# A two-layer hybrid decoder trunk on one core: four reorderings at the joints between stages

## The chip, the core and the metric

The kernel runs on one core of a Trainium2 chip. A core has five engines with their own instruction streams: TensorE (PE in the profile; its weight loads are listed as PEld), VectorE (DVE), ScalarE (ACT), GpSimd (POOL) and SyncE (SP, which here only issues DMAs). They are coupled by semaphores alone. The metric is the device time of one execution in microseconds (us); lower is better.

## The reference

One sequence of 256 tokens with 1024 channels passes through two layers. Each layer is a token mixer and then a channel mixer:

```
h = rms_norm(x) * (1 + scale) + shift
z = h @ w_in                      # conv, stick-breaking q k v, gated linear q k v g, gates
y = g_a * conv(z) @ w_conv_out + g_b * stick(z) @ w_sb_out + g_c * (gla(z) * silu(gg)) @ w_gla_out
x = x + gate * rms_norm(y @ w_o)
x = x + gate * rms_norm(ffn(h2))  # layer 0: dense SwiGLU; layer 1: top-2 of 8 SwiGLU experts
```

The three branches a, b and c are the convolution, the stick-breaking attention and the gated linear attention (GLA). Each is projected to 1024 channels, multiplied by its sigmoid gate, and the three are added ("merged").

## The kernel before

**Products.** Every weight arrives in fp32 as a "unit" of 128 x 2048 values (1 MB), in the order of one list (`plan`, lines 79 to 110), through six raw buffers. ScalarE rounds a unit into a high part (`write_hi`, line 593), VectorE subtracts to get the low part (`write_lo`, line 1002), and TensorE multiplies high weights with high and low activations and low weights with high activations: 48 matmuls of 256 columns, about 5.5 us a unit. A unit's low part is needed only after its first 32 matmuls in most helpers (`low_last`); `project_merged`, which computes the first unit of `w_o`, needs it at once (`begin`). The rounded parts have few slots, so `write_hi` of a unit waits until TensorE is done with an earlier unit.

**Order of a mixer.** Units of one layer's mixer have places i: 0 to 29 are the input projection, 30 to 35 the branch projections ("out", two halves a branch), 36 to 39 `w_o`. Every engine walks the places in its own stream. At place i ScalarE and VectorE first prepare the weights of unit i + 1, and then run a `hook(layer, i)`, where the rest of the mixer's work is placed by hand. At place i VectorE also merges the out unit i - 1 (`merge`, line 1240; `MERGES`): two products of a PSUM bank with the gates (line 1253), and for branch c two further additions into the sum (line 1257). At places 35 and 36 the merge stands ahead of the weights. GpSimd adds the products of branch a to those of branch b, in four pieces q = 0 to 3 (line 568), each as soon as its products are read; the additions of branch c wait for that piece. Pieces 0 and 1 belong to the first halves of the branches, 2 and 3 to the second. ScalarE then rounds merged pieces (line 663), VectorE computes their low parts (line 1304), and TensorE's unit 36 takes them piece by piece (line 1652). Branch c's low and high parts (`split` after the product of line 1299) must be there before TensorE's first unit of branch c; that is the semaphore `c_split`.

**GLA.** At place 21 VectorE cumulates the decays, ScalarE then computes three exponentials (lines 762 to 764), and `gla_decay` (lines 1211 to 1214) multiplies with them; TensorE turns the result at place 23 (line 1852). Between them stand the convolution's taps: at each place up to 26 VectorE adds up to six of them (line 1177). At place 25 VectorE chains the states and TensorE computes GLA's output from them (line 1878).

**Dense layer.** Units are numbered from 0: gate 0, up 0, gate 1, up 1, down 0, ... Units 0 to 2 begin before the norm's scale is known, so VectorE scales units 0 and 1 later (`scale_unit`, line 1134). There are three PSUM banks for such units, so unit 3 needs the bank that `scale_unit` of unit 0 reads.

**Experts.** Eight expert steps of 42 units each. At a step's end TensorE turns the last activations (line 2062), ScalarE rounds them (line 952), VectorE computes their low part (line 1473), and TensorE runs the last two `down` units (line 2050), 24 matmuls of 512 columns. After the eighth step the results are scattered to tokens, normed and stored.

Of the kernel before, what the change touches and what calls it, by code (L numbers as in the profile page):

```python
# [30 lines left out]
P = 128  # L31
# [23 lines left out]
FT = D_FFE // 512  # L55
EU = 6 * FT
# [25 lines left out]
def plan():  # L82
# [4 lines left out]
    for layer in range(DEPTH):  # L87
        later = [("ada", 0, 1, k) for k in range(KC)] + [("ada", 0, 2, k) for k in range(4)]
        for u in range(FIRST if layer == 0 else 0, Z_UNITS + G_UNITS):
            units.append(("z", layer, u, 0))  # L90
            if layer == 0 and u in ADA_AFTER:
                units.append(later.pop(0))
        for b, h in ((1, 0), (1, 1), (0, 0), (0, 1), (2, 0), (2, 1)):
            units.append(("out", layer, b, h))
            if layer == 0 and (b, h) == (1, 0):
                units.append(later.pop(0))
# [109 lines left out]
def program(nc, x_t, vecs, c_row, glr_w, a2, router, stream, experts, out_t):  # L206
    with ExitStack() as ctx:
# [371 lines left out]
        def _(act):  # L579
# [155 lines left out]
            def hook(layer, i):  # L735
# [64 lines left out]
                if i == 31:  # L800
                    for j in range(3):
                        wait_read(act, ("z", layer, Z_UNITS + G_UNITS - 1 - j, 0))
                if i in (31, 32, 34):
                    b = {31: 1, 32: 0, 34: 2}[i]
                    g = gates[:, 8 * b:8 * b + 8, :]
                    act.activation(g, g, ACT.Sigmoid).then_inc(gates_ready, 1)
# [183 lines left out]
        def _(dve):  # L990
# [268 lines left out]
            def hook(layer, i):  # L1259
# [13 lines left out]
                if i == 25:  # L1273
                    gla_states(layer)
                if (4 if layer else FIRST + 1) <= i < 26:
                    taps(layer, i)
# [3 lines left out]
                if i == 21:  # L1280
                    gla_cum(layer)
                if i == 22:
                    gla_decay(layer)
                if i == 27:
# [7 lines left out]
                if i == 30:  # L1292
# [3 lines left out]
                    split(br_hi[0], br_lo[0], conv_tmp, a_split, layer + 1)  # L1296
                if i == 32:
                    dve.wait_ge(gg_silu, layer + 1)
# [41 lines left out]
            for layer in range(DEPTH):  # L1340
# [20 lines left out]
                if layer == 0:  # L1361
                    for i, u in enumerate(FFN_UNITS):
                        if i == 1:
                            finish_mixer_out(0)
                            finish_ffn_in(0)
                            split_shift(layer, SH_F)
                        take(u)
                        if i == 1:
# [3 lines left out]
                        if i == 3:  # L1372
                            scale_unit(FFN_UNITS[0], silu_g[0])
                            scale_unit(FFN_UNITS[1], prod[0])
# [194 lines left out]
        def _(pe):  # L1569
# [469 lines left out]
            def down(step, k, odd, half, t, first=False, last=False, rounds=0):  # L2039
# [17 lines left out]
                mm.then_inc(consumed, 1)  # L2057

            def turn(step, odd, t):
                pe.wait_ge(act_done, step * FT + t + 1)  # L2060
# [37 lines left out]
            def expert_step(step, expert, first=False, again=False, ahead=True):  # L2098
# [18 lines left out]
                if ahead:  # L2117
                    gather(step + 1, 0)
                    gather(step + 1, 1)
                pe.wait_ge(ae_split, step * FT + FT)  # L2120
                for half in range(2):
                    down(step, EU - 2 + half, 0, half, FT - 1, last=True)

# [120 lines left out]
```

## Time and profile before

| | us |
|---|---|
| three executions | 1782.36, 1782.52, 1784.28 |
| their median | 1782.52 |
| the profiled execution, its own time | 1784.1 |
| its span from the first to the last instruction | 1782.4 |
| PE busy | 1757.6 (99%) |
| DVE busy | 1522.5 (85%) |
| ACT busy | 1136.3 (64%) |
| POOL busy | 185.8 (10%) |

The profiled execution's own time is 1.7 us more than its span. Durations below come from it. A row of a timeline gives the start and the length, then engine, line, operation and tiles, how many instructions it merges, and in brackets how long the engine sat idle before it and what released it. Starts of consecutive operations of one engine are closer than their lengths, because the end of one overlaps the start of the next.

### The profile page before, as it was taken

What the parts mean: (1) busy time and instruction counts of PE and PEld (TensorE: products, weight loads), DVE (VectorE), ACT (ScalarE), POOL (GpSimd) and SP (SyncE); (2) the same over time, 40 slices, a digit from 0 to 9 for tenths busy, and PEclk for the clock granted to TensorE, in tenths of its full rate; (3) what the DMA queues carried; (4) which work ended last, traced back from release to release, by engine and by line L of the source; (5) the groups of instructions that cost most, each with busy time, mean ns of one, the idle gap of its engine ahead of it and who ended that gap; (6) DMA issues with size and microseconds to landing.
All of it is one profiled execution on the core that took longest, in us unless ns stands there. A gap on an engine that the chain in (4) does not pass through costs nothing.

```text
span 1782.4 us, 28675 instructions
## 1 busy us (share of the span) xinstructions
PE 1757.6 (99%) x10853; PEld 1557.2 (87%) x10854; DVE 1522.5 (85%) x1444; ACT 1136.3 (64%) x968; POOL 185.8 (10%) x158
## 2 busy tenths in 40 slices
PE   9999999999999999999999999999999999999997
PEld 7999999999999999968888888888888888888885
DVE  7899888999777784769898898898888988988986
ACT  5556476333464556567777777777777776777774
POOL 0395010000029400100000000000000000000000
PEclk9999999999999999999999999999999999999999
DMA  9854655999734343539989989899899899898992
GB/s 386 316 186 160 225 179 217 356 380 375 301 142 166 136 149 142 194 137 361 374 341 372 367 336 382 337 363 371 331 372 376 324 377 369 332 378 341 360 372 96
DMA packets 72820, 524.91 MB, mean 295 GB/s; under 512 B 8145, under 2 KB 8273, under 8 KB 9122
## 3 DMA queue, kind: packets, MB, share of 16 engines
q1 hardware_dynamic: 72578, 523.51, 76.8%
q8 instruction: 61, 1.00, 0.2%
q0 software_dynamic: 160, 0.23, 0.0%
q14 instruction: 21, 0.17, 0.0%
HBM read 522.65 MB, written 1.05 MB: 294 GB/s over the span
## 4 chain that ended last, share of the span: by engine, by line
PE 90%; DVE 5%; ACT 2%; issue 1%; DMA 1%; SPq 0%; DVEq 0%; ACTq 0%
PE bank L2033 34%; PE bank L1635 19%; PE bank L2050 17%; PE bank L1760 3%; PE bank L1717 3%; PE bank L1732 3%; PE bank L2072 2%; PE bank L2062 1%; PE bank L1582 1%; PE bank L1693 1%; DVE w_lo L1002 1%; DVE arena L1177 1%; DVE arena L1253 1%; ACT w_hi L593 1%; DMA raw<-in_stream 1%
## 5 line engine op out<-in xcount | busy, mean ns | idle before, releaser
L1315 DVE TENSOR_TENSOR w_lo<-raw,w_hi 128x2048 fp32r<-128x2048 f32 x224 | 509.8, 2291 | 80.2 <-ACT w_hi L842 79.6
L842 ACT ACTIVATE w_hi<-raw 128x2048 fp32r<-128x2048 f32 x224 | 429.4, 1917 | 99.6 <-PE bank L2050 70.5
L2033 PE MATMUL bank<-acts 128*128 128x512 f32 x1248 | 304.3, 393 | 0.0
L2033 PE MATMUL bank<-w_hi,acts 128*128 128x512 f32 x960 | 297.4, 391 | 0.0
L1315 DVE TENSOR_TENSOR acts<-raw,acts 128x2048 fp32r<-128x2048 f32 x112 | 256.2, 2288 | 21.1 <-ACT acts L842 20.5
L2033 PEld LDWEIGHTS bank<-acts 128*128 128x128 f32 x1248 | 231.3, 188 | 46.7 <-DVE acts L1315 0.4
L842 ACT ACTIVATE acts<-raw 128x2048 fp32r<-128x2048 f32 x112 | 215.0, 1920 | 72.3 <-PE bank L2033 69.9
L2050 PE MATMUL bank<-w_hi,acts 128*128 128x512 f32 x832 | 256.6, 390 | 0.0
L1002 DVE TENSOR_TENSOR w_lo<-raw,w_hi 128x2048 fp32r<-128x2048 f32 x82 | 190.9, 2328 | 41.1 <-ACT w_hi L593 40.8
L593 ACT ACTIVATE w_hi<-raw 128x2048 fp32r<-128x2048 f32 x82 | 156.6, 1912 | 95.1 <-PE bank L1635 66.8
L2033 PEld LDWEIGHTS bank<-w_hi,acts 128*128 128x128 f32 x960 | 179.0, 188 | 36.2
L1635 PE MATMUL bank<-acts,w_hi 128*128 128x256 f32 x1632 | 200.8, 281 | 1.1 <-DVE arena L1134 1.1
L1635 PEld LDWEIGHTS bank<-acts,w_hi 128*128 128x128 f32 x1632 | 193.8, 189 | 3.2 <-issue 2.7
L2033 PE MATMUL bank<-w_lo,acts 128*128 128x512 f32 x480 | 186.9, 389 | 0.0
L2050 PEld LDWEIGHTS bank<-w_hi,acts 128*128 128x128 f32 x832 | 156.6, 188 | 32.5
L2050 PE MATMUL bank<-w_lo,acts 128*128 128x512 f32 x416 | 162.1, 390 | 0.0
L1016 DVE SCALAR_TENSOR_TENSOR raw<-raw,arena 128x1024 f32<-128x1024 f32 x96 | 115.6, 1241 | 15.4 <-DMA raw<-in_stream 10.6
L2033 PEld LDWEIGHTS bank<-w_lo,acts 128*128 128x128 f32 x480 | 90.1, 188 | 18.9
L1635 PE MATMUL bank<-acts,w_lo 128*128 128x256 f32 x816 | 103.1, 279 | 0.0
L1177 DVE SCALAR_TENSOR_TENSOR arena<-arena 128x256 f32<-128x256 f32 x180 | 99.3, 611 | 0.8 <-DVE arena L1227 0.3
L1635 PEld LDWEIGHTS bank<-acts,w_lo 128*128 128x128 f32 x816 | 98.4, 189 | 0.0
L540 POOL TENSOR_SCALAR arena<-arena 128x256 f32<-128x256 f32 x60 | 93.0, 1549 | 0.0
(281 smaller groups left out, 2188.4 us busy)
## 6 DMA issues: line engine op xcount, KB each, us to landing
raw<-in_experts SPq DMA_DIRECT2D x336, 1024.0 KB, 4.9
raw<-in_stream SPq DMA_DIRECT2D x161, 1024.0 KB, 6.4
arena<-in_x_t SPq DMA_DIRECT2D x2, 512.0 KB, 4.6
out_t<-arena SPq DMA_DIRECT2D x4, 256.0 KB, 2.5
arena<-in_vecs SPq DMA_DIRECT2D x1, 224.0 KB, 5.3
arena<-in_glr_w POOLq DMA_DIRECT2D x2, 64.0 KB, 4.7
arena<-in_a POOLq DMA_DIRECT2D x2, 32.0 KB, 5.2
arena<-in_router POOLq DMA_DIRECT2D x1, 32.0 KB, 2.9
```

The lines of the kernel that those rows point to most:

```text
L540: pool.tensor_scalar(product, src, w, None, ALU.mult).then_inc(pool_products, 1)
L593: act.activation(w_hi[SLOT[u]], raw[:, slot, :], ACT.Copy).then_inc(hi_written, 1)
L842: act.activation(expert_hi[s], raw[:, slot, :], ACT.Copy).then_inc(hi_written, 1)
L1002: dve.tensor_tensor(w_lo[SLOT[u]], raw[:, POS[u] % RAW, :], f32(w_hi[SLOT[u]]), ALU.subtract).then_inc(raw_taken, 1)
L1016: ins = dve.scalar_tensor_tensor(w, w, 1.0, cond[row], ALU.mult, ALU.mult, accum_out=ar[:, at:at + 1])
L1177: ins = dve.scalar_tensor_tensor(acc, src, w, acc, ALU.mult, ALU.add)
L1315: dve.tensor_tensor(expert_lo[s], raw[:, slot, :], f32(expert_hi[s]), ALU.subtract).then_inc(raw_taken, 1)
L1635: mm = pe.matmul(out[:, c, :], w[:, 256 * k + P * c:256 * k + P * c + P], h[:, k, :], start=(first and k == 0 and n == 0 and c == 0), stop ...
L1717: mm = pe.matmul(two(bank[c // 2])[:, c % 2, :], w[:, P * c:P * c + P], h[:, k, :], start=(k == 0 and n == 0 and c % 2 == 0), stop=(k == K ...
L1732: mm = pe.matmul(out[:, t, :], h[:, k, P * t:P * t + P], w[:, 256 * k:256 * k + 256], start=(first and t == 0 and k == 0 and n == 0), stop ...
L2033: mm = pe.matmul(bank[b][:, :], (xe_hi if high else xe_lo)[:, c:c + P], w[:, 512 * kk:512 * kk + 512], start=(half == 0 and kk == 0 and n ...
L2050: mm = pe.matmul(bank[5 + d][:, :], (ae_hi if high else ae_lo)[odd][:, c:c + P], w[:, 1024 * f + 512 * d:1024 * f + 512 * d + 512], start= ...
```

## The change

Four edits. (1) The out units of a layer are ordered b, b, a, c, a, c instead of b, b, a, a, c, c; the gate of branch c is computed one place sooner on ScalarE, and the product and split of branch c one place sooner on VectorE. (2) `gla_decay` stands ahead of the taps of place 22. (3) In the dense layer VectorE scales unit 0 ahead of the low weights of unit 3. (4) In an expert step that is not followed by another, the last but one unit is multiplied part by part (all high by high first), TensorE waits only for the high activations before it, and two fp32 matmuls of 512 columns into an unused bank stand ahead of that wait.

```diff
-        for b, h in ((1, 0), (1, 1), (0, 0), (0, 1), (2, 0), (2, 1)):
+        for b, h in ((1, 0), (1, 1), (0, 0), (2, 0), (0, 1), (2, 1)):
...
-                if i in (31, 32, 34):
-                    b = {31: 1, 32: 0, 34: 2}[i]
+                if i in (31, 32, 33):
+                    b = {31: 1, 32: 0, 33: 2}[i]
...
+                if i == 22:
+                    gla_decay(layer)
                 if (4 if layer else FIRST + 1) <= i < 26:
                     taps(layer, i)
...
-                if i == 22:
-                    gla_decay(layer)
...
-                if i == 32:
+                if i == 31:
                     dve.wait_ge(gg_silu, layer + 1)
                     link(dve.tensor_tensor(gla_o, gla_o, gg, ALU.mult))
                     split(br_hi[2], br_lo[2], gla_o, c_split, layer + 1)
...
+                        if i == 3:
+                            scale_unit(FFN_UNITS[0], silu_g[0])
                         take(u)
...
-                            scale_unit(FFN_UNITS[0], silu_g[0])
                             scale_unit(FFN_UNITS[1], prod[0])
...
+            def warm_and_down(step):
+
+                s = moe_begin(step, EU - 2)
+                for _ in range(2):
+                    pe.matmul(bank[7][:, :], ones, area(C_ID, 4 * P), start=True, stop=True)
+                pe.wait_ge(ae_hi_done, step * FT + FT)
+                for n, (w, ae) in enumerate(((expert_hi[s], ae_hi), (expert_lo[s], ae_hi), (expert_hi[s], ae_lo))):
+                    if n == 2:
+                        pe.wait_ge(ae_split, step * FT + FT)
+                    for f in range(2):
+                        for d in range(2):
+                            mm = pe.matmul(bank[5 + d][:, :], ae[0][:, P * f:P * f + P],
+                                           w[:, 1024 * f + 512 * d:1024 * f + 512 * d + 512],
+                                           start=False, stop=False, skip_group_check=True)
+                mm.then_inc(consumed, 1)
...
-                pe.wait_ge(ae_split, step * FT + FT)
-                for half in range(2):
-                    down(step, EU - 2 + half, 0, half, FT - 1, last=True)
+                if ahead:
+                    pe.wait_ge(ae_split, step * FT + FT)
+                    down(step, EU - 2, 0, 0, FT - 1, last=True)
+                else:
+                    warm_and_down(step)
+                down(step, EU - 1, 0, 1, FT - 1, last=True)
```

VectorE's stream in layer 0 at places 21 and 22, before (L1177 are taps, L1211 to L1214 `gla_decay`, L1002 low weights):

```order
L1206 TENSOR_TENSOR arena<-arena 128x1024
L1002 TENSOR_TENSOR acts<-raw,acts 128x2048
L1177 SCALAR_TENSOR_TENSOR arena<-arena 128x256 x6
L1211 COPY arena<-arena 128x16
L1212 TENSOR_TENSOR arena<-arena 128x1024
L1213 TENSOR_TENSOR arena<-arena 128x1024
L1214 TENSOR_TENSOR arena<-arena 128x1024
```

and now:

```order
L1206 TENSOR_TENSOR arena<-arena 128x1024
L1002 TENSOR_TENSOR acts<-raw,acts 128x2048
L1211 COPY arena<-arena 128x16
L1212 TENSOR_TENSOR arena<-arena 128x1024
L1213 TENSOR_TENSOR arena<-arena 128x1024
L1214 TENSOR_TENSOR arena<-arena 128x1024
L1177 SCALAR_TENSOR_TENSOR arena<-arena 128x256 x6
```

The four operations of `gla_decay` have moved ahead of the six taps.

VectorE's stream in layer 0 at places 31 to 33, before (L1253 reads the banks of an out unit, L1299 to L1062 are the product and split of branch c):

```order
L1253 TENSOR_TENSOR arena<-bank6,arena 128x512
L1002 TENSOR_TENSOR w_lo<-raw,w_hi 128x2048
L1253 TENSOR_TENSOR arena<-bank1,arena 128x512
L1253 TENSOR_TENSOR arena<-bank2,arena 128x512
L1299 TENSOR_TENSOR arena<-arena 128x1024
L1061 CAST acts<-arena 128x1024
L1062 TENSOR_TENSOR acts<-arena,acts 128x1024
L1002 TENSOR_TENSOR w_lo<-raw,w_hi 128x2048
```

and now:

```order
L1253 TENSOR_TENSOR arena<-bank6,arena 128x512
L1299 TENSOR_TENSOR arena<-arena 128x1024
L1061 CAST acts<-arena 128x1024
L1062 TENSOR_TENSOR acts<-arena,acts 128x1024
L1002 TENSOR_TENSOR w_lo<-raw,w_hi 128x2048
L1253 TENSOR_TENSOR arena<-bank1,arena 128x512
L1253 TENSOR_TENSOR arena<-bank2,arena 128x512
L1002 TENSOR_TENSOR w_lo<-raw,w_hi 128x2048
```

The product and split of branch c stand ahead of the low weights of unit 33 instead of behind the merge of unit 31.

VectorE's stream in layer 0 from the merge of unit 33 to the low weights of unit 36, before (L1257 adds branch c to the sum):

```order
L1253 TENSOR_TENSOR arena<-bank5,arena 128x512
L1253 TENSOR_TENSOR arena<-bank6,arena 128x512
L1253 TENSOR_TENSOR arena<-bank0,arena 128x512
L1257 TENSOR_TENSOR arena<-arena 128x512
L1253 TENSOR_TENSOR arena<-bank1,arena 128x512
L1257 TENSOR_TENSOR arena<-arena 128x512
L1002 TENSOR_TENSOR w_lo<-raw,w_hi 128x2048
```

and now:

```order
L1253 TENSOR_TENSOR arena<-bank5,arena 128x512
L1257 TENSOR_TENSOR arena<-arena 128x512
L1253 TENSOR_TENSOR arena<-bank6,arena 128x512
L1257 TENSOR_TENSOR arena<-arena 128x512
L1253 TENSOR_TENSOR arena<-bank0,arena 128x512
L1253 TENSOR_TENSOR arena<-bank1,arena 128x512
L1002 TENSOR_TENSOR w_lo<-raw,w_hi 128x2048
```

The four operations of branch c's first half now come first, and branch a's two last ones directly precede the low weights of unit 36. Layer 1 has the same pieces.

## Rows read from the trace of the kernel before

**Rows 1.** The page: each engine's busy time, share of the span and instructions.

```profile
PE 1757.6 (99%) x10853; PEld 1557.2 (87%) x10854; DVE 1522.5 (85%) x1444; ACT 1136.3 (64%) x968; POOL 185.8 (10%) x158
```

**Rows 2.** Waits of TensorE's weight loads, both layers: us in total, times, longest.

```profile
PEld bank L1652 <- DVE w_lo L1002: 3.6, 2, 1.8
```

**Rows 3.** Timeline of layer 0 around `gla_decay` and the states, places 22 to 25.

```profile
167.93 1.04 ACT L764 ACTIVATE arena<-arena 128x1024 f32<-128x1024 f32 x1
168.10 2.46 DVE L1177 SCALAR_TENSOR_TENSOR arena<-arena 128x256 f32<-128x256 f32 x6
170.48 0.17 DVE L1211 COPY arena<-arena 128x16 f32<-128x16 f32 x1
...
174.48 0.85 PEld L1852 LDWEIGHTS bank<-arena 128*128 128x128 f32 x8 [0.91 <-DVE arena L1214]
...
176.55 3.29 DVE L1177 SCALAR_TENSOR_TENSOR arena<-arena 128x256 f32<-128x256 f32 x6
...
190.40 0.52 PEld L1878 LDWEIGHTS bank<-arena 128*128 128x128 f32 x4
```

**Rows 4.** Timeline of layer 0, places 31 to 34: VectorE, TensorE and ScalarE.

```profile
234.86 1.29 DVE L1253 TENSOR_TENSOR arena<-bank,arena 128x512 f32<-128x512 f32 x2 [1.40 <-ACT arena L806]
...
238.46 3.70 PEld L1745 LDWEIGHTS bank<-acts,w_hi 128*128 128x128 f32 x32
...
240.02 1.21 DVE L1299 TENSOR_TENSOR arena<-arena 128x1024 f32<-128x1024 f32 x1
...
243.26 2.29 DVE L1002 TENSOR_TENSOR w_lo<-raw,w_hi 128x2048 fp32r<-128x2048 f32 x1
...
244.27 1.92 ACT L593 ACTIVATE w_hi<-raw 128x2048 fp32r<-128x2048 f32 x1 [3.51 <-PE bank L1745]
```

**Rows 5.** The same stretch, VectorE beside GpSimd's additions, to unit 36.

```profile
245.47 1.28 DVE L1253 TENSOR_TENSOR arena<-bank,arena 128x512 f32<-128x512 f32 x2
...
246.30 1.31 POOL L568 TENSOR_TENSOR arena<-arena 128x512 f32<-128x512 f32 x1 [66.56 <-DVE arena L1253]
...
246.66 3.09 DVE L1002 TENSOR_TENSOR w_lo<-raw,w_hi 128x2048 fp32r<-128x2048 f32 x1
...
251.59 1.14 DVE L1257 TENSOR_TENSOR arena<-arena 128x512 f32<-128x512 f32 x1
...
254.35 2.28 DVE L1002 TENSOR_TENSOR w_lo<-raw,w_hi 128x2048 fp32r<-128x2048 f32 x1
...
256.56 1.28 DVE L1304 TENSOR_TENSOR acts<-arena,acts 128x512 fp32r<-128x512 f32 x2
...
257.76 0.68 DVE L1253 TENSOR_TENSOR arena<-bank,arena 128x512 f32<-128x512 f32 x1
```

**Rows 6.** Timeline of layer 1: a GpSimd operation and VectorE's next one.

```profile
653.43 2.79 POOL L559 TENSOR_SCALAR_AFFINE_SELECT arena<-arena 128x1024 f32<-128x1024 f32 x1 [52.51 <-ACT arena L772]
...
655.19 1.31 DVE L1177 SCALAR_TENSOR_TENSOR arena<-arena 128x256 f32<-128x256 f32 x1
```

**Rows 7.** Timeline at the start of the dense layer, units 3 and 4.

```profile
309.23 1.41 DVE L1134 TENSOR_TENSOR arena<-bank,arena 128x512 f32<-128x512 f32 x2
...
310.03 3.71 PEld L1635 LDWEIGHTS bank<-acts,w_hi 128*128 128x128 f32 x32 [1.28 <-issue]
...
314.38 0.69 DVE L1062 TENSOR_TENSOR acts<-arena,acts 128x512 fp32r<-128x512 f32 x1
...
315.48 5.82 PEld L1760 LDWEIGHTS bank<-acts 128*128 128x128 f32 x48
```

**Rows 8.** The last expert's end: timeline; one stretch (length, busy, granted clock); fp32 matmuls.

```profile
1756.96 0.60 ACT L952 ACTIVATE acts<-bank 128x512 fp32r<-128x512 f32 x1 [1.18 <-PE bank L2062]
...
1758.81 4.19 PE L2050 MATMUL bank<-acts 128*128 128x512 f32 x12 [1.88 <-DVE acts L1473]
...
1760.30:1763.70 3.40, 3.40 (x10) 2.63 (x9) 0.00 (x0) 0.00 (x0) 0.00 (x0) 0.50 0.02 5
...
L1592 PE MATMUL bank<-arena 128*128 128x512 f32 x10 | 4.6, 592 | 0.0
```

## The prediction, on record before the changed kernel ran

> **What bounds the kernel now.** I read the page first: TensorE is busy 99% of the span [rows 1], so only its few pauses can be won, and whatever makes it pause costs its full length. Next its waits: the longest that this change touches is 1.8 us before unit 36, once in each layer, for low weights [rows 2]. Then the timeline around each edit, to see what is late next. The whole gain open to it, in weight-load time, is 2 x 1.8 us there, 0.91 us before GLA's turn [rows 3], 1.28 us before dense unit 3 [rows 7], and at the end 1.88 us of pause with the slow clock behind it [rows 8]. All times below are shifts of TensorE.
>
> **Decay ahead of taps (layer 0).** TensorE waits 0.91 us for the last decay product [rows 3]. VectorE is free at 168.10, where the taps start, but the third exponential ends on ScalarE at 167.93 + 1.04 = 168.97, and `gla_decay` waits for all three. So it starts near 169.03, not 170.48, and ends at 172.98 instead of 174.43; TensorE no longer waits there (it is through at 174.48 - 0.91 = 173.57). But VectorE has now stood idle for 169.03 - 168.10 = 0.93 us, and up to the states it has no other idle time: the same operations follow back to back until `gla_states`, for whose end TensorE's output products wait at 190.40, just as TensorE gets there. VectorE ends 0.93 us later, plus about 0.15 us because GpSimd's mask operation, which stretched the taps from 2.46 to 3.29 us [rows 3], now meets them nearer their start. TensorE thus goes on at 191.48 instead of 190.40: **+1.1 us**, after a pause of 1.1 + 0.9 = 2.0 us. Bounds: +0.8 (the mask meets no tap) and +1.2. In layer 1 fewer taps stand there and, by the same timeline, the states are ready about 2 us before TensorE asks; the 0.9 us fit in: 0.
>
> **Branch c sooner (each layer).** After the first merge at 234.86 (1.20 us), the product and split take 243.26 - 240.02 = 3.24 us [rows 4], so `c_split` comes at 239.30. TensorE wants unit 33 at 238.46 [rows 4] and now needs it there: a new pause of 0.86 us. It is later absorbed, since unit 36 waits anyway; what counts is VectorE's chain to unit 36. I lay it out in layer 0. Low weights take 2.20 us from start to start, a merge of two operations 1.20, one of four 2.65 when undisturbed. From 239.30: low weights of 33, merge of 31, low weights of 34, merge of 32, at 246.10. The high weights of 35 wait for unit 33 to end, so they move by TensorE's 0.86 us from 244.27 + 1.92 [rows 4] to 247.05: VectorE idles 0.99 us.
>
> Then GpSimd. Its addition takes 1.31 us alone; VectorE's low weights issued 0.36 us behind one took 3.09 us, and 2.28 us where GpSimd was at rest; an addition from SBUF took 1.14 us, while reads of a bank kept their length [rows 5]. GpSimd's operation at 653.43 took 2.79 us behind low weights, and the tap that VectorE had next, at 655.19, took 1.31 us: it stood behind the waiting GpSimd, which went first [rows 6]. So these take turns in whole operations, in the order of asking. With 1.20 us less before it, GpSimd's first addition starts at 245.74 and its second at 247.01, 0.08 us ahead of VectorE's low weights of 35 at 247.09. These wait: next operation at 250.39 (1.10 us of blocking). Merge of c to 253.04, merge of a's second half to 254.24. That merge now starts GpSimd's last two additions at 253.86, right in front of the low weights of 36, which take 3.0 us as in rows 5: to 257.22 (0.78 blocked). GpSimd's last addition, waiting since, goes ahead of the low parts of line 1304 (1.11 blocked). The last merge starts at 259.53 instead of 257.76 [rows 5]. In numbers: waits and blocking before were 0.56 + 0.82 + 0.45 + 0.39 = 2.22 us, now 0.99 + 1.10 + 0.78 + 1.11 = 3.98. **+1.76 us** at the last merge, on which TensorE's third and fourth pieces of unit 36 and the high weights of 37 hang. Unit 36 itself starts at 257.36 (before: 256.69), so the low weights that the edit means to bring sooner come later. Layer 1 has the same distances: twice, **+3.5 us**. Bounds per layer: if VectorE gets ahead of GpSimd's second addition at 247.09, 0.99 + 0.38 + 0.78 + 1.11 = 3.26, +1.04; if the two shared in proportion, without whole turns, +0.4; if no operation were slowed, 0.99 - 2.22 = -1.2.
>
> A page of the Trainium skill speaks against this edit: "SBUF — State Buffer", section Who interferes with whom, says that a VectorE instruction with two SBUF inputs and a GpSimd instruction that reads SBUF exclude each other for whole instructions, the first to start going first, and that VectorE with one SBUF input is free. Rows 5 and 6 agree. By that rule the edit costs +1.76 us a layer, by a shared bandwidth it would cost +0.4.
>
> **Bank read ahead of low weights (dense layer).** VectorE is free at 307.03, so it reads unit 0's bank at once, and TensorE starts unit 3 near 308.8 instead of 310.03 [rows 7]. But unit 4 needs the first dense activations, whose low part ends at 314.38 + 0.69 = 315.07 behind the same VectorE work in another order. It starts at 315.13 instead of 315.48: **-0.35 us**; the other 0.9 us become a wait there. Bounds 0 and -1.2.
>
> **The last down units.** TensorE starts at 1758.81, after low activations; the high ones end at 1756.96 + 0.60 = 1757.56 [rows 8]. The two fp32 matmuls take 0.43 us each by 4.6 us for ten [rows 8], starting at 1756.8, so they end at 1757.66, and the first product starts near 1757.73: **-1.1 us**. Eight matmuls cover the low activations (1758.70). The rounded and low weights of both units are there. In this execution the clock then stood at 1.2 instead of 2.4 GHz for 3.40 us [rows 8]; kept at 2.4 GHz it gives another **-1.7 us**. All that follows moves along.
>
> **Sum.** Against the profiled execution (1784.1): +1.1 + 3.5 - 0.35 - 1.1 - 1.7 = +1.5, so 1785.6. Against the median (1782.52) the clock needs care: two executions lie at 1782.4 to 1782.5, the third and the profiled one 1.7 us above, which is the slow clock's price. I take it that the median had no slow stretch, and only +1.1 + 3.5 - 0.35 - 1.1 = +3.15 applies: 1785.7. Both ways meet; I say **1785.6**, 0.17% slower, which is within 0.2% (3.6 us), about what a measurement of this kernel can tell from no change. Of the clock a page of the skill, "TensorE: Matmul & The Clock Gate", What's actually happening, says that one kernel shows different numbers of slow matmuls from run to run; the three times fit, no second profile shows it here.
>
> **Rivals.**
> Slower: the clock falls in the new pauses. The 1.88 us pause at the end brought 1.2 GHz [rows 8], the 1.8 us ones before unit 36 did not. New are 2.0 us before GLA's output, and in each layer 1.65 us before unit 36 with 0.8 us more inside it. Each fall costs 1.7 us: one in the median execution makes 1787.3, two 1789.0. It decides from 1786.1, that is from one fall on. Chance 0.30 (one 0.22, more 0.08).
> GpSimd comes second: a margin of 0.08 us is small, and the order of waiting rests on one pair of rows. Then +1.04 or +0.4 a layer and 1782.9 to 1784.2; I give 0.27.
> It works as meant: low weights of 36 in time, branch c hidden, decay and bank pauses gone: -3.6 - 0.9 - 1.3 - 1.1 = -6.9, 1775.6. Against it stand VectorE's chains above, which have no idle time to give. 0.05.
> The forecast, 1784.9 to 1786.3, has 0.38.
>
> **Numbers.** Slower by over 0.2% (above 1786.1): 0.30 and a quarter of the forecast's 0.38, 0.39. Faster: 0.05. Within: 0.56. The range leaves out about 0.1 on each side: the best part of the second and all of the third rival below 1782.2, two falls of the clock above 1788.2.
>
> **What the profile after would show.** TensorE waiting about 0.9 us for the split at the fourth out unit, in both layers; 1.65 us before unit 36; GpSimd's additions with 3 us low weights beside the last two; 2.0 us before line 1878 in layer 0 and none before line 1852; the wait at unit 3 gone and 0.9 us at unit 4; the last down units starting 1.2 us after the turn at 2.4 GHz. It would be wrong if the low weights of 36 end before TensorE asks, or if VectorE's operations keep their lengths beside GpSimd.

## The result

The changed kernel takes 1786.12 us in the median (1785.72 to 1787.19), the kernel before 1782.57 us, both over 20 executions; the ratio is 1.0017 with a 95% interval of 1.0011 to 1.0023. The forecast was 1785.6. So the change makes the kernel slower, by 3.0 us by the ratio and 3.6 us by the medians.

The 20 times of the kernel before lie in two groups, 13 between 1781.9 and 1782.9 and 7 between 1783.8 and 1784.6, the changed kernel's in one. What follows compares with the lower group, about 1782.5, where nothing else is said; why there are two is the subject of the section on the end.

The profiled execution of the changed kernel took 1786.77 us, with a span of 1784.9. Its page has this row (busy time, share, instructions), to hold against [rows 1]:

```profile
PE 1760.7 (99%) x10857; PEld 1559.1 (87%) x10858; DVE 1525.0 (85%) x1444; ACT 1135.9 (64%) x968; POOL 183.4 (10%) x158
```

The busy times say nothing: the loss is 2.5 us of span. The waits of TensorE's weight loads (us in total, times, longest) say where to look, against [rows 2]:

```profile
PEld bank L1653 <- DVE w_lo L1002: 3.2, 2, 1.6
...
PEld bank L1653 <- DVE acts L1304: 1.6, 3, 0.7
PEld bank L1879 <- DVEq L1231: 1.6, 1, 1.6
PEld bank L1746 <- DVE acts L1062: 1.6, 2, 0.8
```

(Lines of the changed kernel are one higher from the dense layer's edit on, and 17 higher behind the new function.) The wait for the low weights of unit 36 is nearly as long as before, and three others are new or longer: the states before GLA's output, the split of branch c before the fourth out unit (both new), and the low parts of merged pieces within unit 36 (1.6 us in place of 0.5).

The same weight loads in the two profiled executions, changed kernel against kernel before:

| at | before, us | changed, us | later by |
|---|---|---|---|
| line 1852 / 1853, decayed operands turned, layer 0 | 174.48 | 173.60 | -0.88 |
| line 1891 / 1892, behind GLA's output | 200.60 | 201.60 | +1.00 |
| line 1582 / 1583, first norm behind the mixer | 274.42 | 277.66 | +3.24 |
| line 1760 / 1761, dense unit 4 | 315.48 | 318.47 | +2.99 |
| line 1842 / 1843, before GLA's decays, layer 1 | 625.16 | 628.13 | +2.97 |
| line 2014 / 2015, behind layer 1's mixer | 776.34 | 780.88 | +4.54 |
| line 2062 / 2079, last turn | 1756.32 | 1760.89 | +4.57 |
| the last down product | 1765.77 | 1768.31 | +2.54 |

Read from top to bottom: edit 2 costs 1.0 us, edit 1 costs 2.2 us in layer 0 and 1.57 us in layer 1, edit 3 gives 0.25 us, and the end gives 2.03 us against this execution of the kernel before, which had the slow clock there.

**Decay.** Timeline of the changed kernel, against [rows 3]:

```profile
169.10 0.18 DVE L1211 COPY arena<-arena 128x16 f32<-128x16 f32 x1 [0.82 <-ACT arena L764]
...
173.60 0.90 PEld L1853 LDWEIGHTS bank<-arena 128*128 128x128 f32 x8
...
188.26 3.03 DVE L1227 SCALAR_TENSOR_TENSOR arena<-arena,bank 128x128 f32<-128x128 f32 x8
...
191.40 0.52 PEld L1879 LDWEIGHTS bank<-arena 128*128 128x128 f32 x4 [1.59 <-DVEq L1231]
```

VectorE idles 0.82 us for the third exponential, TensorE turns without waiting, and then waits 1.59 us for the states, which end at 191.29.

**Branch c.** Timeline of layer 0, against [rows 4, 5]:

```profile
239.05 1.22 DVE L1062 TENSOR_TENSOR acts<-arena,acts 128x1024 fp32r<-128x1024 f32 x1
...
240.33 3.71 PEld L1746 LDWEIGHTS bank<-acts,w_hi 128*128 128x128 f32 x32 [0.79 <-DVE acts L1062]
...
246.75 2.55 POOL L568 TENSOR_TENSOR arena<-arena 128x512 f32<-128x512 f32 x2 [67.59 <-DVE arena L1253]
248.10 3.34 DVE L1002 TENSOR_TENSOR w_lo<-raw,w_hi 128x2048 fp32r<-128x2048 f32 x1 [0.91 <-ACT w_hi L593]
...
254.02 1.28 DVE L1253 TENSOR_TENSOR arena<-bank,arena 128x512 f32<-128x512 f32 x2
254.84 4.58 POOL L568 TENSOR_TENSOR arena<-arena 128x512 f32<-128x512 f32 x2 [5.55 <-DVE arena L1253]
255.22 3.06 DVE L1002 TENSOR_TENSOR w_lo<-raw,w_hi 128x2048 fp32r<-128x2048 f32 x1
...
258.20 2.37 DVE L1304 TENSOR_TENSOR acts<-arena,acts 128x512 fp32r<-128x512 f32 x2
258.33 0.53 PEld L1653 LDWEIGHTS bank<-acts,w_hi 128*128 128x128 f32 x4 [1.60 <-DVE w_lo L1002]
...
260.50 0.68 DVE L1253 TENSOR_TENSOR arena<-bank,arena 128x512 f32<-128x512 f32 x1
```

Every VectorE operation with two SBUF operands that meets a GpSimd addition is long here: low weights 3.34 and 3.06 us where 2.28 us is their length alone, the pair of line 1304 2.37 us where 1.28 is. The last merge begins at 260.50; less the 1.0 us from above that is 259.50, 1.74 us later than the 257.76 of [rows 5].

**Dense layer.** The bank is read at once, and the wait is now at unit 4 [rows 7]:

```profile
310.37 0.68 DVE L1134 TENSOR_TENSOR arena<-bank,arena 128x512 f32<-128x512 f32 x1
...
318.47 3.65 PEld L1761 LDWEIGHTS bank<-acts 128*128 128x128 f32 x30 [0.72 <-DVE acts L1062]
```

**The end.** Timeline of TensorE, against [rows 8]; line 2064 is the warming, line 2071 the new product order:

```profile
1760.89 0.60 PE L2079 MATMUL bank<-arena 128*128 128x128 f32 x4
1761.33 1.88 PE L2064 MATMUL bank<-arena 128*128 128x512 f32 x4
1762.64 3.33 PE L2071 MATMUL bank<-acts 128*128 128x512 f32 x12
```

And two stretches (length, busy times, then the granted clock as a share of 2.4 GHz, DMA share, GB/s), the second of which is in unit 36 of layer 0:

```profile
1762.00:1769.50 7.50, 7.03 (x30) 5.05 (x28) 2.10 (x4) 1.47 (x4) 0.00 (x0) 1.00 0.02 4
...
260.30:263.70 3.40, 3.40 (x18) 3.40 (x18) 3.33 (x6) 1.07 (x2) 0.00 (x0) 0.50 0.66 275
```

The last units now run at 2.4 GHz, but in this execution the clock fell to 1.2 GHz for 3.4 us behind the pauses around unit 36. From GLA's output to the first norm, line 1891 to line 1582, edit 1 alone costs 1.55 us with the clock held (200.43 to 275.80, against 200.60 to 274.42); here it is 2.24 us. The fall therefore cost 0.69 us, not the 1.7 us that 3.4 us at half the clock would take, because it ran through waits that TensorE would have had. With edit 1 alone these two stand there, and the changed kernel has neither:

```profile
261.45 0.53 PEld L1652 LDWEIGHTS bank<-acts,w_hi 128*128 128x128 f32 x4 [0.69 <-ACT acts L663]
...
262.72 1.00 PEld L1652 LDWEIGHTS bank<-acts,w_hi 128*128 128x128 f32 x8 [0.27 <-DVE acts L1304]
```

1.7 less 0.69 and 0.27 is 0.74 us. The fall also agrees with this execution taking 0.65 us more than the median.

### The profile page after: what moved, and what is told of

It reads as the page before. It is cut to its first block, busy times and chain, and to the rows that moved or that the text cites. A ratio compares the mean times of both kernels' runs of the same rounds, so it can differ in the third digit from the quotient of the medians.

```text
span 1784.9 us, 28682 instructions
## 1 busy us (share of the span) xinstructions
PE 1760.7 (99%) x10857; PEld 1559.1 (87%) x10858; DVE 1525.0 (85%) x1444; ACT 1135.9 (64%) x968; POOL 183.4 (10%) x158
## 4 chain that ended last, share of the span: by engine, by line
PE 91%; DVE 6%; ACT 2%; issue 1%; DMA 0%; DVEq 0%; ACTq 0%
PE bank L2034 34%; PE bank L1636 18%; PE bank L2051 17%; PE bank L1761 3%; PE bank L1718 3%; PE bank L1733 3%; PE bank L1583 2%; PE bank L2089 2%; PE bank L2079 1%; DVE arena L1177 1%; PE bank L1694 1%; DVE w_lo L1002 1%; PE bank L1746 1%; ACT w_hi L593 1%; DVE arena L1253 1%
## 5 line engine op out<-in xcount | busy, mean ns | idle before, releaser
L1002 DVE TENSOR_TENSOR w_lo<-raw,w_hi 128x2048 fp32r<-128x2048 f32 x82 | 193.0, 2354 | 41.7 <-ACT w_hi L593 41.3
L1177 DVE SCALAR_TENSOR_TENSOR arena<-arena 128x256 f32<-128x256 f32 x180 | 99.3, 611 | 0.8 <-DVE arena L1227 0.3
```

The source lines that it names most:

```text
L1002: dve.tensor_tensor(w_lo[SLOT[u]], raw[:, POS[u] % RAW, :], f32(w_hi[SLOT[u]]), ALU.subtract).then_inc(raw_taken, 1)
L1177: ins = dve.scalar_tensor_tensor(acc, src, w, acc, ALU.mult, ALU.add)
```

## The experiments

The four edits alone come first. Edit 1 alone has the first part of the change's diff, and nothing else; likewise the others.

### Edit 1 alone

```diff
-        for b, h in ((1, 0), (1, 1), (0, 0), (0, 1), (2, 0), (2, 1)):
+        for b, h in ((1, 0), (1, 1), (0, 0), (2, 0), (0, 1), (2, 1)):
...
-                if i == 32:
+                if i == 31:
                     dve.wait_ge(gg_silu, layer + 1)
```

> The kernel before with edit 1 alone (branch c's first half one unit sooner). Theory (VectorE and GpSimd exclude each other for whole operations, and the chain of VectorE to unit 36 is full): the last merge of unit 36 comes 1.7 us later in each layer, TensorE 1.5 to 1.8 us a layer, so +3.1 to +3.5 us against a kernel before without a slow stretch at the end. Rival (only the new pause of 0.8 us before the fourth out unit is passed on): +1.6 us.

Measured: 1787.40 us in the median of 9 (1785.49 to 1788.30), ratio 1.0022 (1.0012 to 1.0032). The nine, too, lie in groups, and here most are in the upper one: three at 1785.5 to 1786.6, six at 1787.3 to 1788.3, in the mean 3.4 and 3.6 us above the group of the kernel before that each answers to. In the profiles TensorE loses 1.55 us in layer 0 up to the first norm and 1.60 us in layer 1: 3.15 us in all, the lower end of what was expected; the times give its upper end. Another 0.30 us is lost between the norm and dense unit 4, but this is not edit 1's: that stretch takes 41.06 us in the profile of the kernel before and up to 41.36 us in others with the same code there, with edit 1 and without. The timeline of layer 0:

```profile
246.84 1.30 POOL L568 TENSOR_TENSOR arena<-arena 128x512 f32<-128x512 f32 x1
246.94 3.34 DVE L1002 TENSOR_TENSOR w_lo<-raw,w_hi 128x2048 fp32r<-128x2048 f32 x1 [0.92 <-ACT w_hi L593]
...
259.34 0.68 DVE L1253 TENSOR_TENSOR arena<-bank,arena 128x512 f32<-128x512 f32 x1
```

GpSimd's second addition begins at 246.84, 0.10 us ahead of the low weights, which then take 3.34 us: the order on which the prediction rested, and nearly its margin of 0.08 us.

### Without GpSimd's additions

Two kernels leave out GpSimd's eight additions, one of them without edit 1 and one with it; the sum then lacks branch a's products, and the signals stay.

```diff
-                    pool.tensor_tensor(m, m, gates[:, 2 * q:2 * q + 2, :], ALU.add).then_inc(branch_added, 1)
+                    pool.sem_inc(branch_added, 1)
```

> The kernel before without GpSimd's eight additions of branch a's products to branch b's (the signals stay, the sum lacks branch a). Theory (lock for whole operations): VectorE's low weights take 2.3 us throughout, its additions 0.69; the 0.82 + 0.45 + 0.39 us of blocking are gone, so the last merge comes up to 1.7 us sooner in each layer and TensorE 1.2 to 1.7 us: -2.4 to -3.4 us in all. Rival (GpSimd has no part in it): 0.

> The same without GpSimd's additions, with edit 1. Theory: edit 1 then costs only its additional idling of VectorE, 0.3 to 0.5 us a layer, so +0.6 to +1.0 us over the run without the additions and without edit 1. Rival (the new pause before the fourth out unit is the cost): +1.6 us. Rival (blocking by GpSimd is no part): +3.1 us.

Measured: 1780.59 us (ratio 0.9980, 0.9971 to 0.9989) without edit 1, and 1780.53 us (0.9985, 0.9976 to 0.9994) with it. The medians mislead, since six of ten times of the one and four of ten of the other are in an upper group. Lower groups: 1778.8 to 1779.4 and 1779.9 to 1780.6, so edit 1 now costs 1.1 us, little more than the 0.6 to 1.0 expected. The profiles give 0.40 us in layer 0 up to the first norm and 0.43 in layer 1 between the two kernels. The experts' data differ in these kernels, but not their time: from line 2014 to the last turn TensorE takes 979.8 us without edit 1, as in the kernel before, and 981.0 with it, where the clock fell once (last section). Timelines of layer 0, first without edit 1:

```profile
246.37 2.28 DVE L1002 TENSOR_TENSOR w_lo<-raw,w_hi 128x2048 fp32r<-128x2048 f32 x1
...
252.41 2.28 DVE L1002 TENSOR_TENSOR w_lo<-raw,w_hi 128x2048 fp32r<-128x2048 f32 x1
...
254.75 0.53 PEld L1652 LDWEIGHTS bank<-acts,w_hi 128*128 128x128 f32 x4 [0.20 <-DVE w_lo L1002]
...
255.82 0.68 DVE L1253 TENSOR_TENSOR arena<-bank,arena 128x512 f32<-128x512 f32 x1
```

and with it:

```profile
239.20 3.83 PEld L1745 LDWEIGHTS bank<-acts,w_hi 128*128 128x128 f32 x32 [0.79 <-DVE acts L1062]
...
253.23 2.28 DVE L1002 TENSOR_TENSOR w_lo<-raw,w_hi 128x2048 fp32r<-128x2048 f32 x1
...
256.15 0.55 PEld L1652 LDWEIGHTS bank<-acts,w_hi 128*128 128x128 f32 x4
256.63 0.68 DVE L1253 TENSOR_TENSOR arena<-bank,arena 128x512 f32<-128x512 f32 x1
```

With GpSimd silent every low-weights operation takes 2.28 us, and unit 36 waits 0.20 us or not at all. The pause before the fourth out unit is still 0.79 us with edit 1, and yet the edit costs only 0.4 us a layer. So of edit 1's 1.55 and 1.60 us a layer, 1.15 us each go when GpSimd is silent; the new pause is no more than a part of the rest. And the kernel before itself pays for its eight additions 1.60 us (layer 0, to the first norm) and 1.59 us (layer 1), 3.2 us by the profiles and 3.4 by the lower groups.

### Edit 1 with the low weights of unit 36 first

```diff
-                    if i in (LATE - 1, LATE):
+                    if i == LATE:
                         merge(layer, MERGES[i], units[MERGES[i]])
...
-                    if i < LATE - 1 and i in MERGES:
+                    if i < LATE and i in MERGES:
                         merge(layer, MERGES[i], units[MERGES[i]])
```

> Edit 1 alone, and the low weights of unit 36 ahead of the merge of branch a's second half, which with edit 1 stands directly before them and starts GpSimd's last two additions. Theory (the sum of turns on VectorE's chain counts, not where unit 36 begins): the low weights take 2.3 us and the pause of 1.6 us before unit 36 goes, but GpSimd's last two additions now start 2.3 us later and block the low parts of the merged pieces, so the last merge comes within 0.4 us of where it was with edit 1 alone; TensorE waits inside unit 36 instead, and the time is that of edit 1 alone within 1 us. Rival (the pause before unit 36 is the cost): 1.6 us a layer come back, 3.2 us faster than edit 1 alone.

Measured: 1786.19 us in the median of 10 (ratio 1.0020, 1.0011 to 1.0030), with groups at 1785.8 to 1786.3 and 1787.3 to 1788.3, where edit 1 alone has 1785.5 to 1786.6 and 1787.3 to 1788.3. In the profiles TensorE loses 1.54 and 1.77 us, 3.3 in all, against 3.15. Timeline of layer 0 (this execution runs 0.5 us later than that of edit 1 alone from before the edit on):

```profile
253.36 2.29 DVE L1002 TENSOR_TENSOR w_lo<-raw,w_hi 128x2048 fp32r<-128x2048 f32 x1
...
255.99 0.53 PEld L1652 LDWEIGHTS bank<-acts,w_hi 128*128 128x128 f32 x4
256.39 2.97 POOL L568 TENSOR_TENSOR arena<-arena 128x512 f32<-128x512 f32 x2 [7.75 <-DVE arena L1253]
...
258.27 1.00 PEld L1652 LDWEIGHTS bank<-acts,w_hi 128*128 128x128 f32 x8 [1.30 <-DVE acts L1304]
...
259.83 0.68 DVE L1253 TENSOR_TENSOR arena<-bank,arena 128x512 f32<-128x512 f32 x1
...
261.95 0.54 PEld L1652 LDWEIGHTS bank<-acts,w_hi 128*128 128x128 f32 x4 [1.46 <-ACT acts L663]
```

The pause of 1.6 us ahead of unit 36 is gone: the unit begins the moment TensorE is free. It then waits 1.30 and 1.46 us inside, because the last merge begins at 259.83 - 0.5 = 259.3, just where it was. The longest of the waits at unit 36 was not what cost the time.

### Edit 2 alone, and with six taps moved

Edit 2 alone:

```diff
+                if i == 22:
+                    gla_decay(layer)
                 if (4 if layer else FIRST + 1) <= i < 26:
                     taps(layer, i)
...
-                if i == 22:
-                    gla_decay(layer)
```

The other kernel moves, in layer 0, the six taps of place 24 behind the states of place 25 as well:

```diff
-                if (4 if layer else FIRST + 1) <= i < 26:
+                if i == 22:
+                    gla_decay(layer)
+                if (4 if layer else FIRST + 1) <= i < (26 if layer else 24):
                     taps(layer, i)
+                if layer == 0 and i == 25:
+                    taps(layer, 24)
+                    taps(layer, 25)
```

> The kernel before with edit 2 alone (gla_decay ahead of the taps of place 22). Theory (VectorE's 0.93 us of idling before the decay comes out at the states, since it has no other idle time up to them): TensorE waits 1.6 us before the output products of layer 0 and not at all before turning the decayed operands; +1.0 us in layer 0, 0 in layer 1. Rival (the time before the states is slack): -0.9 us.

> Edit 2 alone, and in layer 0 the six taps of place 24 moved behind the states of place 25. Theory (the states are late because VectorE has no idle time before them): they now end 2.4 us sooner, TensorE waits neither before turning the decayed operands nor before the output products, and since VectorE has 4 to 5 us of idling right behind, the taps end as before: -0.7 to -0.9 us against the kernel before, 1781.6 without a slow stretch at the end. Rival (the states wait for something else, TensorE's own products): +0.9 us as with edit 2 alone.

Measured: 1783.32 us (1.0004, 0.9995 to 1.0013) and 1782.15 us (0.9997, 0.9988 to 1.0006). Neither interval leaves 1. The lower groups differ as expected (medians of about 1783.3 and 1782.0, against 1782.6 and 1782.5 of the kernel before beside each), and the profiles decide. TensorE's weight loads for GLA's output with edit 2 alone, and then with the moved taps:

```profile
191.04 0.52 PEld L1878 LDWEIGHTS bank<-arena 128*128 128x128 f32 x4 [1.39 <-DVEq L1231]
```

```profile
190.12 0.53 PEld L1881 LDWEIGHTS bank<-arena 128*128 128x128 f32 x4
```

With edit 2 alone TensorE turns the decayed operands 1.0 us sooner than before and is 0.65 us late behind GLA (201.25 against 200.60), having waited 1.39 us. With the taps out of the way it waits at neither place and is through 0.75 us sooner, once the 0.48 us are taken off by which this execution was late already at 155.8. The kernel before's own profile is a little slow here: it takes 44.81 us from 155.79 to 200.60, the nine other profiles without edit 2 44.59 to 44.69. Over the same stretch edit 2 alone takes 45.52, the changed kernel 45.71, and the moved taps 44.06. So edit 2 costs 0.7 to 0.9 us alone and 0.9 to 1.1 us in the changed kernel, and with the taps moved it gains 0.55 to 0.75 us. In layer 1 edit 2 changes nothing: it is 0.77 us late at line 1842 (625.93 against 625.16) and 0.77 at GLA's turn there.

### Edit 3 alone

```diff
+                        if i == 3:
+                            scale_unit(FFN_UNITS[0], silu_g[0])
                         take(u)
...
-                            scale_unit(FFN_UNITS[0], silu_g[0])
```

> The kernel before with edit 3 alone (unit 0's bank read ahead of the low weights of unit 3). Theory: the wait of 1.3 us at dense unit 3 goes, one of 0.7 to 0.9 us appears at unit 4 for the low part of the first dense activations; -0.35 us, which the comparison can hardly tell from nothing, so the profile decides: start of unit 4 in relation to the norm. Rival (the wait just moves whole): 0.

Measured: 1782.83 us (0.9999, 0.9990 to 1.0008); five of the eleven times are at 1781.7 to 1782.1, five in an upper group at 1783.2 to 1783.7, one between. By the profile the pause at unit 3 is gone, one of 0.72 us stands before unit 4, and TensorE gains 0.25 us between the first norm and unit 4 (-0.26 to -0.51 against the kernel before); in the changed kernel it is the same (+3.24 to +2.99). Across all fourteen profiles this stretch takes 40.81 or 40.82 us in the three with edit 3 and 41.06 to 41.36 us in the eleven without, so the sign is clear and the gain is 0.25 to 0.55 us. It is below what the times can tell.

### The end: edit 4 with two, one and no warming matmul, and warming alone

Edit 4 alone is the last part of the change's diff. The next two differ from it in `warm_and_down`, with one turn of this loop, and without the loop:

```diff
-                for _ in range(2):
+                for _ in range(1):
                     pe.matmul(bank[7][:, :], ones, area(C_ID, 4 * P), start=True, stop=True)
```

The fourth is the kernel before with only this:

```diff
+                if not ahead:
+                    for _ in range(2):
+                        pe.matmul(bank[7][:, :], ones, area(C_ID, 4 * P), start=True, stop=True)
                 pe.wait_ge(ae_split, step * FT + FT)
```

> The kernel before with edit 4 alone. The profile after shows four passes of 0.43 us for the two fp32 matmuls, where I had counted two. Theory: they end 0.85 us after the high activations are there and so delay the first product; TensorE goes on 0.3 to 0.4 us sooner than before, and the clock keeps 2.4 GHz in the last down units in every execution. So -0.35 us against executions of the kernel before at about 1782.3, -1.7 to -2.1 against those at about 1784.2, and no second group of times. Rival (warming has nothing to do with the clock, falls come with the phase of something else): two groups of times 1.7 us apart, as with the kernel before.

> The kernel before with edit 4, without its two warming matmuls. Theory: the first product starts 0.8 to 0.9 us sooner than with warming, 1.2 us sooner than in the kernel before, and the remaining pause of about 0.9 us is too short to bring the slow clock: -1.2 us against executions of the kernel before at about 1782.3. Rival (it is the pause however short, and the warming is what keeps the clock): a second group of times 1.7 us above, in which a stretch of 3.4 us at 1.2 GHz stands in the last down units.

> The kernel before with edit 4, but one warming matmul instead of two. Theory: its two passes of 0.43 us end as the high activations arrive, so the first product starts like without warming (within 0.1 us): 1781.4 to 1781.5, no second group of times. Rival (any warming delays): between the runs with two and with none, 1781.7.

> The kernel before with the two warming matmuls alone, ahead of its wait for the low activations of the last step. Theory: four passes of 0.43 us fit into the pause of 1.88 us, nothing is delayed (0 to +0.05 us), and the slow clock no longer appears: all executions at 1782.2 to 1782.9, none at 1784. Rival (the clock falls by something else): a third of the executions still at 1784.

| kernel | times, us (11 executions) | median, ratio with interval | turn to last down product, us |
|---|---|---|---|
| edit 4 (two warming matmuls) | 1781.56 to 1783.19 | 1781.94, 0.9995 (0.9986 to 1.0004) | 7.41 |
| with one | 1781.02 to 1781.91 | 1781.45, 0.9991 (0.9982 to 1.0000) | 6.63 |
| with none | 1781.05 to 1782.72 | 1781.45, 0.9991 (0.9982 to 1.0000) | 6.71 |
| warming alone | 1782.16 to 1783.36 | 1782.51, 0.9997 (0.9988 to 1.0006) | 7.78 |

The last column is the time from the start of the last turn to the start of the last product of the last down unit, in the profile. Without edit 4 and without warming it is 7.79 to 7.82 us in the four profiles in which the clock held there (edits 2 and 3 alone, the moved taps, edit 1 without additions) and 9.38 to 9.45 us in the four in which it fell there (the kernel before with and without additions, edit 1 alone and with the low weights first). So the fall costs 1.6 us, and edit 4 is worth 0.4 us as built and 1.1 to 1.2 us with one warming matmul or none. TensorE's timeline with one, and with none:

```profile
1756.48 0.60 PE L2078 MATMUL bank<-arena 128*128 128x128 f32 x4
1756.92 1.02 PE L2063 MATMUL bank<-arena 128*128 128x512 f32 x2
1757.77 3.01 PE L2070 MATMUL bank<-acts 128*128 128x512 f32 x12
```

```profile
1756.36 0.60 PE L2076 MATMUL bank<-arena 128*128 128x128 f32 x4
1757.73 3.00 PE L2068 MATMUL bank<-acts 128*128 128x512 f32 x12 [0.78 <-ACT acts L952]
```

One fp32 matmul is two rows (x2 for one, x4 for two), each 0.43 us from start to start. One fits in the wait for the high activations; two overrun it. In the changed kernel the first product's row begins at 1762.64, but the second product starts 0.64 us later instead of 0.23, so the first was still held up, as the warming from 1761.33 on would do with four times 0.43 us (to 1763.05).

Warming alone, ahead of the old wait: the timeline, and the granted clock from the first product on, which held to the end of the down units:

```profile
1757.02 1.88 PE L2122 MATMUL bank<-arena 128*128 128x512 f32 x4
1759.07 2.97 PE L2050 MATMUL bank<-acts 128*128 128x512 f32 x12 [0.17 <-DVE acts L1473]
```

```profile
1758.90:1762.30 3.40, 3.23 (x15) 2.74 (x15) 0.07 (x1) 0.00 (x0) 0.00 (x0) 1.00 0.02 5
```

It delays nothing (2.48 us from turn to first product, 2.49 before), and 10 of its 11 times lie between 1782.1 and 1782.9, the last at 1783.36, while of the kernel before's 33 beside it 14 lie above 1783.6. So the upper group of the kernel before is the clock's fall in the last down units. Over all its executions on record 40 of 117 lie in that group, 7 of 20, 11 of 31, 14 of 33 and 8 of 33. Nearly the same as with warming holds without: only one of 11 times stands out, with a pause of 0.98 us in place of 2.09. In the profiles of these four kernels the weight loads pause here for 0.98 us at most at a time, whether the pause was filled or cut, and the clock holds; lengths between that and 2.09 us were not tried.

### The parts that pay, together

Edit 2 with the moved taps, edit 3, and edit 4 without warming; edit 1 is left out.

> Edit 2 with the moved taps, edit 3, and edit 4 without warming; edit 1 left out. Theory (the parts add up): -0.8 - 0.4 - 0.95 = -2.15 us against executions of the kernel before without a slow stretch (1782.4), 1780.3, and no second group of times from the end. Rival (edit 3's gain is lost as the stages before it are shifted): 1780.7.

Measured: 1780.44 us in the median of 11 (1780.02 to 1781.52), ratio 0.9987 (0.9978 to 0.9996), faster than both kernels. In the profile TensorE is 0.77 us ahead behind GLA, 0.24 us more in the dense layer (-0.95 to -1.19), and 1.1 us more at the end (6.71 us from turn to last product): the parts add up, and edit 3's gain is not lost. Two of the eleven times still stand about 1 us above the others; why is not shown.

## Why the prediction was right

It was right in its mechanisms; the step at the end was mis-sized, and part of the closeness is luck (see the sum). Point by point:

**Decay, +1.1 us.** 1.0 us in the changed kernel against the profile of the kernel before, 1.1 against the nine others; 0.7 and 0.9 alone. The operations stand within 0.1 us of where they were put (169.10 against 169.03). The forecast's 0.15 us for the mask operation did not come: the taps beside it take 3.29 us as before. The same stretch varies by 0.2 us between profiles with the same code, which is the precision of this term. The chain behind it is shown: with six taps out of it, the loss becomes a gain.

**Branch c, +1.76 us a layer.** 1.55 and 1.60 us alone, 1.57 in layer 1 of the changed kernel. The last merge was forecast 1.77 us later and came 1.74 later; TensorE did not lose all of it. The order in which GpSimd and VectorE take their turns was forecast operation by operation and holds. By the Trainium skill's page "SBUF — State Buffer", section Who interferes with whom, VectorE with two SBUF inputs contends with a GpSimd instruction that reads SBUF, and with one such input it does not. The rows agree: the pair that reads a bank at 254.02 keeps its 1.28 us beside the addition at 254.84, and the operations with two SBUF operands are long. The runs without the additions make it more than an argument: GpSimd's turns are 1.15 us of the cost in each layer. The bound for no slowing at all, -1.2 us a layer, is met as well: edit 1 without the additions stands 1.20 us (layer 0) and 1.16 us (layer 1) better than the kernel before with them.

**Bank read, -0.35 us.** -0.25 us against the profile of the kernel before, in three profiles, and up to -0.55 against the others. The wait at unit 4 is 0.72 us where 0.9 was forecast.

**The end, -1.1 us.** This step failed in size: 0.4 us. "The two fp32 matmuls take 0.43 us each by 4.6 us for ten" read 0.43 us as the price of one matmul, but the ten instructions of that group were passes, two to a matmul, as the four rows for two matmuls show. The warming takes 1.72 us, not 0.86, and outlasts the high activations (there at 1762.13 in the changed kernel) by 0.9 us. With one or none the full 1.1 us appear.

**The clock, -1.7 us against executions in which it falls.** 1.6 us, and it falls in about a third of the kernel before's executions, so the median did not have it, as assumed. The Trainium skill's page "TensorE: Matmul & The Clock Gate", What's actually happening, says that the same kernel measures different numbers of slow matmuls at its start from run to run; here the difference stands at the kernel's end, in the two groups of times. The forecast said that this part would bring nothing against the median; it brings a narrower spread.

**The sum.** With the measured terms: 1.0 + 1.55 + 1.57 - 0.25 - 0.4 = +3.5 us against the lower group, 1785.9 to 1786.0; measured 1786.1, in executions of which some have a fall of the clock. The forecast's +3.15 was 0.3 us short of these terms, because two errors partly cancelled: the warming was priced 0.7 us too low, and branch c 0.4 us too high. The result lies at the very edge of what the forecast called within 0.2% (up to 1786.1).

**Rivals.** That the clock falls in the new pauses did happen in the profiled execution, in unit 36, at 0.69 us instead of the 1.7 that the rival priced: where an engine is about to wait anyway, running at half rate costs only what exceeds the wait. In the other 19 executions only the mean granted clock is on record. Beside the experiments the kernel before has 0.997 in 23 of its 33 executions of the upper group and in none of the 64 others; the changed kernel has 0.997 in seven of twenty, the profiled one among them, 0.46 us above the mean of the other thirteen. So falls probably came in a third of its executions or more, and the median most likely has none; where they came in those is not shown. GpSimd did not come second, though its margin was only 0.1 us, in layer 0 of all three profiles with edit 1 and the additions; the low weights behind it are as long in layer 1 (3.34 or 3.35 us). Nothing worked as meant except the dense layer's edit and the cutting of the last pause.

## What to carry to other kernels

Where a side engine shares an exclusive path with the engine that carries the chain, count its operations as part of that chain, in the order in which both ask, and look at what each earlier step now starts in front of. Where a wait vanishes upstream or downstream of a full chain it comes back at the next dependence: neither the low weights first nor the decay first bought anything, and the decay did once taps were taken out from ahead of the consumer. Before adding filler work to a pause, read from the trace how many rows one such instruction makes and how long the pause is that remains, not the one that was there.

## What the runs showed of the hardware that was not expected

- An fp32 matmul of 512 columns is two entries of 0.43 us each from start to start at 2.4 GHz, 0.86 us together (the two of the warming are four rows, and PE has 10857 in place of 10853); one of the rounded type (fp32r) is one entry of 0.23 us.
- A pause of 2.1 us in TensorE's weight loads, in a stream that is otherwise 99% busy, was followed by 3.4 us at 1.2 GHz in the profile of the kernel before, and by the groups of times in 40 of its 117 executions and in six of nine of edit 1 alone. What decides between the two is not shown. The length of the pause alone does not: the two of 1.8 us before unit 36 brought no fall in the kernel before, nor did one of 2.0 us at line 1582 in layer 1 with three more of 0.34 to 0.73 us behind it; one of 1.6 with 0.7 us more behind it did, once, in the changed kernel.
- The clock also fell at another place once, with edit 1 and no additions, behind the short pauses before layer 1's experts (length, busy times, granted clock, DMA share, GB/s):

```profile
774.00:778.00 4.00, 3.81 (x24) 3.84 (x25) 1.27 (x7) 1.19 (x2) 0.00 (x0) 0.57 0.00 0
```

- The same fall costs 1.6 us in the last down units, 1.2 us before the experts (981.0 us in place of 979.8 from there to the last turn), and 0.69 us in unit 36, where TensorE has waits behind it.
- Blocked time is inside the length of a row: GpSimd's addition of 1.29 us shows as 3.33 us (from 256.09 on in the changed kernel) while VectorE's low weights hold it off, so here a long row on either engine is a sign of the other, not of more work.
